# Moving the issue of the expert down weights from SyncE to ScalarE in a one-core MoE block

## The reference

```
v   = rmsnorm(h, g_ffn)                       # (512, 1024)
combine = top-1 of 4 groups x top-2 of 8 experts of it, as weights
for each of the 32 experts e:
    hg = silu(v @ w_gate[e]) * (v @ w_up[e])  # w_gate, w_up: (1024, 256)
    h += combine[:, e] * (hg @ w_down[e])     # w_down: (256, 1024)
```

## Time and profile before

| | us |
|---|---|
| median of 3 runs | 566.22 (564.44 to 569.38) |
| the profiled execution | 568.34 |
| its span, first to last instruction | 566.7 |
| PE busy | 486.8 |
| ACT busy | 151.3 |
| transfers of the SP queue | 133.89 MB of 142.85 MB |

### The profile page before, as it was taken

One profiled execution on the slowest core, in us unless ns is written; L12 is line 12 of the kernel. 1 busy time (PEld: TensorE's weight loads), 2 busy tenths in 40 slices (PEclk: granted clock), 3 DMA queues, 4 the chain that ended last, 5 costly groups with the idle time before them and its releaser, 6 DMA issues.

```text
span 566.7 us, 6991 instructions
## 1 busy us (share of the span) xinstructions
PE 486.8 (86%) x2649; PEld 281.0 (50%) x2649; DVE 236.5 (42%) x641; ACT 151.3 (27%) x247; POOL 158.3 (28%) x136
## 2 busy tenths in 40 slices
PE   4799999799999993499999969778788878699993
PEld 3356777334844483355555545545455553344441
DVE  4899888995132555222322221111222100253434
ACT  6243444634343221011111110110111013412463
POOL 1069999913120000222322211102210111001450
PEclk9799999969999995599999998888999989879997
DMA  8764100794295748179999999999999994810011
GB/s 310 138 149 102 31 1 2 204 124 152 83 409 228 304 173 363 35 269 418 419 419 418 416 417 424 420 419 419 419 422 420 420 416 202 323 48 1 0 74 74
DMA packets 53950, 142.85 MB, mean 252 GB/s; under 512 B 27504, under 2 KB 32636, under 8 KB 40988
## 3 DMA queue, kind: packets, MB, share of 16 engines
q1 hardware_dynamic: 48620, 133.89, 63.6%
q0 software_dynamic: 4896, 8.47, 4.1%
q10 hardware_dynamic: 400, 0.04, 0.1%
HBM read 136.57 MB, written 14.19 MB: 266 GB/s over the span
## 4 chain that ended last, share of the span: by engine, by line
PE 84%; issue 5%; DVE 4%; ACT 2%; DMA 2%; POOL 1%; SPq 0%; POOLq 0%; DVEq 0%
PE bank L1361 77%; PE bank L1618 3%; PE bank L1632 1%; PE bank L1564 1%; PE bank L1436 1%; DMA h<-in_x_dram 1%; DVE ut L733 1%; DMA moe<-v_d,gidx_all 1%; DVE moe L733 1%; DVE moe L749 0%; POOL zbuf L1267 0%; DVE ring L733 0%; ACT ut L485 0%; ACT ring L477 0%; DVE ut L984 0%
## 5 line engine op out<-in xcount | busy, mean ns | idle before, releaser
L1361 PE MATMUL bank<-ring,moe 128*64 128x256 f32 (+3 forms) x1136 | 150.9, 410 | 20.5 <-issue 17.5
L1361 PEld LDWEIGHTS bank<-ring,moe 128*64 128x64 f32 (+1 forms) x1136 | 94.1, 150 | 61.8 <-issue 35.5
L1290 POOL DMA_INDIRECT pairs_d<-ut,sidx_all x32 | 31.9, 996 | 182.8 <-ACT ut L473 113.2
L733 DVE TENSOR_TENSOR moe<-moe,bank 64x128 f32<-64x128 f32 x64 | 18.6, 291 | 145.4 <-ACT moe L664 144.4
L1361 PE MATMUL bank<-ut,big 128*128 128x512 f32 x128 | 60.0, 618 | 3.6 <-ACT ut L485 3.6
L664 ACT ACTIVATE moe<-bank 64x256 f32<-64x256 f32 x32 | 12.1, 377 | 178.3 <-PE bank L1361 178.3
L1361 PE MATMUL bank<-big,ut 128*128 128x512 f32 x128 | 58.8, 619 | 0.9 <-ACT ut L603 0.9
L1361 PE MATMUL bank<-ring,ut 128*128 128x512 f32 x128 | 57.8, 611 | 1.4 <-DVE ut L733 1.4
L1361 PE MATMUL bank<-big,moe 128*64 128x256 f32 (+1 forms) x280 | 48.6, 440 | 9.6 <-issue 8.3
L1361 PEld LDWEIGHTS bank<-big,ut 128*128 128x128 f32 x128 | 25.2, 199 | 33.6 <-issue 33.3
L733 DVE TENSOR_TENSOR ring<-ring,bank 128x64 f32<-128x64 f32 (+1 forms) x142 | 39.5, 278 | 2.8
(11 more groups left out here) (167 smaller groups left out, 526.2 us busy)
## 6 DMA issues: line engine op xcount, KB each, us to landing
ring<-in_exp_w_gate_dram SPq DMA_DIRECT2D x22, 1024.0 KB, 23.3
ring<-in_exp_w_up_dram SPq DMA_DIRECT2D x22, 1024.0 KB, 28.4
ring<-in_exp_w_down_dram SPq DMA_DIRECT2D x22, 1024.0 KB, 27.3
big<-in_exp_w_gate_dram SPq DMA_DIRECT2D x10, 1024.0 KB
big<-in_exp_w_up_dram SPq DMA_DIRECT2D x5, 1024.0 KB
big<-in_exp_w_down_dram SPq DMA_DIRECT2D x5, 1024.0 KB, 29.1
zbuf<-in_exp_w_up_dram SPq DMA_DIRECT2D x5, 1024.0 KB
zbuf<-in_exp_w_down_dram SPq DMA_DIRECT2D x5, 1024.0 KB
```

The source lines that it names most:

```text
L733: return dve.tensor_tensor(o, a, b, op)
L1290: pool.indirect_dma_start(pairs, bass.IndirectOffsetOnAxis(ap=index, axis=0), at(ut, ALL, k * 512, [[1, 512]]), None, bounds_check=4 * T - ...
L1361: return pe.matmul(o, a, b, start=start, stop=stop, skip_group_check=loose)
```

## The change

ACT issues the down weights of experts 6 to 31 (pieces 20, 23, ..., 95: 26 transfers of 1 MiB), each right behind its copy of the down product of the expert six before, on its own queue. It has waited for `dn_ps` there already. SP issues gate and up of these experts and no longer waits for `dn_ps` in its loop. Slots, sizes, semaphores and the order of work on PE, DVE and POOL are the same. The first 18 pieces are issued by SP as before.

```
@@ -429,8 +429,9 @@
                 weights(sp, p)
             for p in range(NPIECE, 3 * NE):
                 e, k = (p - NPIECE) // 3, (p - NPIECE) % 3
-                sp.wait_ge(gu_ps if k < 2 else dn_ps, e + 1)
-                weights(sp, p)
+                if k < 2:
+                    sp.wait_ge(gu_ps, e + 1)
+                    weights(sp, p)
 
             with sp.If(most(sp) > CAP):
                 with sp.Fori(1, ROUNDS) as r:
@@ -668,6 +669,8 @@
                 act.wait_ge(dn_ps, e + 1)
                 least(act, ys_stored[e % YBUF], e // YBUF * 16)
                 copy(at(ut, ALL, e % YBUF * 512, [[1, 512]]), bank[4 + e % 2][:, :], dn_sb)
+                if 3 * e + 2 + NPIECE < 3 * NE:
+                    weights(act, 3 * e + 2 + NPIECE)
 
             silu(0)
             for e in range(NE):
```

## The result

The changed kernel takes 570.42 us (median of 20 runs, 567.34 to 572.34) against 566.63 us (20 runs, 564.44 to 569.38): ratio 1.0058, 95% interval 1.0042 to 1.0075, +3.3 us. The forecast was 569.0 us, +0.5%, from 564.3 to 573.6.

What follows compares the result with a forecast made beforehand. The prediction took DMA to bound the expert stage from 323 us on. Its terms, -1.3 + 0 + 2.5 + 1.6 + 0 = +2.8 us, put on the median of 566.2, gave 569.0 us (+0.5%), range 564.3 to 573.6.

Steps and rivals of the forecast that it cites:

- What bounds the kernel: Expert stage: PE bounds it up to 323 us, DMA from then on, at 416 to 424 GB/s.
- Part 1: Near the start, SP no longer waits for the down product, so the DMA gap closes: -1.3 us, bounds -1.6 and 0.
- Part 2: Issuing 26 down pieces on ACT costs 0.33 us each in its free time: 0, bounds 0 and +1.8 us.
- ACT is held by the full queue: Rival: ACT's issue takes some 7 us, silu is late by 3.7 us, giving 572.7 us; chance 0.11.
- SP's issues would get short again: Sign: SP's issues, 2 to 5 us each later in the kernel before, get short again.
- (a): End of experts: up 31 becomes the last byte of the weights, one piece later: +2.5 us.
- (b): Last three or four experts: gate and up land faster than PE computes, so PE falls behind: +1.6 us (0.9 to 2.3).
- (c): Toward the end: a block at the low clock takes 7.08 us instead of 5.39; put at 0, upper bound +1.7.
- Behind the experts: Both paths to the gate, over PE and over the combined pairs, and the end are later by 2.8 us.
- The order of landing stays as it was: Rival: DMA engines serve both issuers in order of issue, only the closed gap is left: 564.9 us; chance 0.17.
- Two queues move more: Rival: two queues feed the DMA engines better from 245 to 467 us; 1.2% more rate gives 566.3 us; chance 0.12.
- Down pieces starve: Rival: ACT's queue gets well under a third of the rate, down pieces gather, +10.8 us, 577.0 us; chance 0.05.

Runs made afterwards that it cites:

- e3: Changed kernel, but SP issues the down pieces of the last six experts in the old place, ACT those of experts 6 to 25; ratio 0.9988 against before.
- e8: Kernel before, with POOL waiting for the down pieces of experts 10 and 23 and writing one word each; one profiled execution, 566.92 us.
- e2: Changed kernel, but SP again waits for the down product of e - 1 before gate and up of e + 6; ratio 1.0112 against before.
- e5: Changed kernel, but SP issues the down piece of expert 31 alone, behind gate and up of expert 31; ratio 1.0013 against before.
- e6: Changed kernel, but from expert 18 on ACT issues a down piece three experts before its use instead of six; ratio 1.0039 against before.
- e4: Changed kernel, but SP issues the down pieces of experts 6 to 25 in the old order, ACT only the last six; ratio 1.0079 against before.
- e7: Changed kernel, with POOL waiting for the down pieces of experts 10 and 23; run once, no ratio; they landed 10.2 and 9.5 us after issue.
- e1: Kernel before, SP issuing all pieces, but gate and up of expert e + 7 ahead of down of e + 6; ratio 0.9994 against before.

## Why the prediction was right

**What bounds the kernel.** Right. The rate did not move, and PE's slack in the middle is shown by e3 (waits begin early at no cost) and e8.

**Part 1, the gap: -1.3 us.** It measures 1.6 us (e2 against the changed kernel, pairs combined), or 1.9 us (the changed kernel against before), 1.7 us by the means of the two groups in the table: at or a little over the upper bound of the working.

**Part 2, ACT's issue: 0.** Right, and the rival that ACT is held by the full queue falls: 0.33 to 0.35 us each, also at 249.6 us and later while SP is held for 8.5 us. That SP's issues would get short again was wrong: they became fewer and some longer. Gate and up landed later still than the 35 us that I gave: up 28 was issued at 403.52 us and the block that waited for it started at 447.50 us, 44.0 us on, where it had been 28.8 us before (411.83 to 440.66).

**Part 3 (a), one piece later: +2.5 us.** Shown by e5 (2.5 us by the ratios, 2.35 in the profiles) and by the last wait of e6. e3 and e4 show that the whole cost lies in the last six experts.

**Part 3 (b) and (c), catching up: +1.6 us, and blocks at the low clock: 0, bound +1.7.** These are the mis-sized terms, in opposite directions. The three blocks without waits are there in every profile of the changed kernel, where three or four were forecast; they come every 5.89 us (447.50 to 465.18 us), not every 6.02, since no gathered rows are turned (L1621) ahead of the last two. At what pace gate and up landed there no row shows. In its two profiles with a fast block behind the last wait (229.24 and 228.71 us, mean 229.0) the last down product is 1.6 us later than in the two of before (mean 227.3); with the gap of 1.6 added and the 2.5 of (a) taken off, 0.7 us are left for (b). In e7, which differs only in its marks, that block took 7.08 us:

```profile
444.22 3.43 issue
447.65 7.08 PE bank L1367 x40
```

and the last down product is at 231.25 us, 3.9 us later than before, so (b) and (c) are 3.0 us together. I had named a slow block behind the last wait as the upper bound, +1.7, and put it at 0, because waits get fewer; but the last of them is now followed by blocks with no slack, where a slow one adds its full 1.7 us; e2 shows the same. How often this happens over 20 runs no profile here says; the ratio leaves 3.3 + 1.6 - 2.5 = 2.4 us for both, e4's +4.5 us less 2.5 leaves 2.0 (its own profile has only +2.9 at the last down product), and I had 1.6.

The sum with measured terms is -1.6 + 2.5 + 0.7 = +1.6 us with a fast block and +3.9 with a slow one; the ratio says +3.3 (2.4 to 4.2), between them. That the sum of +2.8 came so near is in part luck: 0.9 us too much in (b) and nothing for (c) cancel.

**Behind the experts** the shift was handed on whole, as forecast, but one step of the reasoning was wrong: both paths to the gate were to be 2.8 us later. The pairs were combined 1.9 us sooner (245.41 against 247.30), which fits the closed gap, since all bytes are through sooner, while the last down product was 1.8 us later. It did no harm, since the later path decides. e1 showed the limit of the sentence: it holds for a later PE and not for an earlier one.

**The rivals.** "The order of landing stays as it was" falls by e7. "Two queues move more" falls by the flat 418 to 421 GB/s. "Down pieces starve" falls: no wait stands ahead of a down product.

## What to carry to other kernels

When a stage is bound by transfers, ask of each reordering which piece becomes the last byte and how much work hangs on it; e5 shows that one piece of 78 can carry three quarters of the effect. A second queue is not only issue time: its pieces overtake. Giving the short queue to the pieces that are needed first would be the next thing to try; no run here did. Before a gain on one path is booked, look for the path beside it: here 0.4 us separated the two, and a gain of 3.9 us on PE became 1.4 us at the gate.

## What was not expected

SP's queue can be full and hold SP for 8.5 us while an issue on ACT's queue takes 0.33 us. A piece on the short queue took 9.5 us with hardly another beside it in that queue, where an equal share of the rate would give 5.0 us plus latency. The clock of the block behind a wait doesn't follow from the length of the wait alone: 2.64 us was followed by a block of 5.39 us (granted clock 1.00) in the changed kernel, 2.31 us by one of 7.08 us (0.76) in e2.
